# Gated MLPs of a two-block kernel: high weights against both halves of the input in 512-column products

## The chip, the cores and the metric

One core of one Trainium2 chip runs the whole program. The metric is the device time of one execution in microseconds (us), as the median of several runs; less is better. Times inside a run come from one execution that the hardware profiler recorded.

## The reference

The program computes two transformer blocks on 256 tokens of width 1024, in float32. The first has two layers of attention and squared-ReLU MLPs. The second has a gated MLP, a mixer (a state-space part beside latent attention) and another gated MLP. The two gated MLPs are what matters here:

```python
def swiglu(h, w_gate, w_up, w_down):          # h: 256 x 1024
    return (silu(h @ w_gate) * (h @ w_up)) @ w_down    # hidden width D_FF_2 = 2816
x = x + 0.5 * g1 * swiglu(modulate(rmsnorm(x, ...), sh1, sc1), ffn1_w_gate, ffn1_w_up, ffn1_w_down)
...
x = x + 0.5 * g3 * swiglu(modulate(rmsnorm(x, ...), sh3, sc3), ffn2_w_gate, ffn2_w_up, ffn2_w_down)
```

## The kernel before

**Split numbers.** TensorE multiplies in the type fp32r. To keep float32 accuracy, each operand is split into a high part (rounded to fp32r) and a low part (the rest), and a product is the sum of three: high weight with high input, high weight with low input, low weight with high input. The input's halves stand in `ah` and `al`, 8 tiles of 128 channels by 256 tokens each.

**Units.** Weights stream through in units of 1 MB (128 partitions by 2048 values) in a ring of three slots. The sync engine loads a unit into `raw` (`load`), ScalarE copies it into `whi` (`split`, L610), VectorE subtracts for `wlo` (`split`, L1065). A unit's slot is used again when TensorE has counted up `w_used`. Each engine works through its own queue in the order written.

**A gated MLP** (`swiglu` in each of the three engines' programs) has 11 chunks of 256 hidden channels. A chunk has a gate unit, an up unit and a down unit, and TensorE takes them in the order gate(j+1), up(j+1), down(j). A gate or up unit is an `a_unit`: 2 blocks of 128 output channels (m) by 8 input tiles (c) by 3 products, each of 256 columns, into one bank of PSUM (8 banks of 512 values per partition); the two blocks are the halves of that bank. Gate and up of one chunk go into banks 4 and 5, those of the next chunk into 6 and 7. The first gate and up unit are `entry_unit` and `up_unit`, which start on parts of the input. The down unit is `d_unit` (L1949, L1951, L1953): 24 products of 512 columns, in which weights are streamed and parts of h stand still, alternating between two banks; the last two down units are `last_pair` (L1913), which finishes one bank after another.

**Between the units** (`chunk`): ScalarE takes Silu of the gate bank into `hr` (L826); VectorE multiplies it with the up bank into `hs` (L1418); ScalarE copies `hs` to the high part `hh` (L828); VectorE subtracts for the low part `hl` (L1423), which releases the down unit. On both engines this stands between the weight splits of the following units: gate(j+2)'s before it, up's and down's behind it. In the first gated MLP VectorE also does the last norm of the first block (`final_norm`, written behind the first two chunks) and, two chunks on, the angles of the mixer (`angles`).

`gained` writes `ah` and `al` at the entry of a stage, with casts (L1144) and subtractions (L1145) of two tiles at once.

Of the kernel before, what the change touches and what calls it, by code (L numbers as in the profile page):

```python
# [15 lines left out]
P = 128  # L16
# [94 lines left out]
def build(nc, t_in, out):  # L111
    g = t_in
    with ExitStack() as ctx:
        def sb(name, shape, dt=F32):
            return ctx.enter_context(nc.sbuf_tensor(name, shape, dt))

        def sem(name):
            return ctx.enter_context(nc.semaphore(name))
# [3 lines left out]
        wlo = sb("wlo", [P, RING, UNIT], F32R)  # L122
        x = sb("x", [P, TT, D])
        xn = sb("xn", [P, TT, D])
        ah = sb("ah", [P, CT, S], F32R)
        al = sb("al", [P, CT, S], F32R)
        bh = sb("bh", [P, CT, S], F32R)
        bl = sb("bl", [P, CT, S], F32R)
        hh = sb("hh", [P, MLP_BODY, 2, S], F32R)
# [34 lines left out]
        place = sb("place", [P, 32 + 2 * 96])  # L164
        ps = ctx.enter_context(nc.psum_tensor("ps", [P, 8, 512], F32))

        wflat = work[:]
        hr = wflat[:, 0:512]
        hs = wflat[:, 512:1024]
# [29 lines left out]
        rope = wflat[:, 1024:2048].rearrange("p (k n) -> p k n", k=4)  # L199
        rB = gB[:, 0:S]  # L200
        rdiag = wflat[:, 1024:1024 + S].rearrange("p (t n) -> p t n", t=TT)
        fscr = st[:, 0:4096].rearrange("p (k n) -> p k n", k=8)
        nac = sm[:, 7, :].rearrange("p (t h) -> p t h", t=TT)

# [65 lines left out]
        pv_done = sem("pv_done")  # L270
        o_ready = sem("o_ready")
        gated = sem("gated")
        h_sq = sem("h_sq")
        half_tr = sem("half_tr")
        half_hi = sem("half_hi")
# [90 lines left out]

        def bank(b, n=512):
            return ps[:, b, 0:n]

        def banks(b, n):  # L370
            return ps[:].rearrange("p b n -> p (b n)")[:, 512 * b:512 * b + n]
# [229 lines left out]
        def _(act):  # L601
# [132 lines left out]
            def plain(h0, j, dst):  # L734

                act.wait_ge(pv_done, h0 + 4 * (j + 1))
                A.activation(dst.rearrange("p c n -> p (c n)"), bank(4 + j % 2), ACT.Copy).then_inc(in_hi, 1)

            def head_exp(hg, h, src, scale):
                act.wait_ge(maxed, hg + 1)  # L740
# [77 lines left out]
            def chunk(cs, used_units, b, silu, buf):  # L818
# [10 lines left out]
                else:  # L829
                    A.activation(hr, bank(b), ACT.Relu).then_inc(gated, 1)  # L830
                    act.wait_ge(gated, cs1)
                    A.activation(hh[:, buf].rearrange("p c n -> p (c n)"), hr, ACT.Square).then_inc(h_hi, 1)

            def mlp(n0, c0):
                def body(i):
                    for j in range(MLP_BODY):
                        chunk(i * MLP_BODY + (c0 + j), up_end(n0, i, j, 2, MLP_BODY), 4 + j, False, j)
                        for q in range(2):
                            n = n0 + 2 * j + 2 + q
                            split(n if isinstance(i, int) else (n, i), slot(n))  # L840
                body(0)
                with act.Fori(1, (CH1 - 1) // MLP_BODY) as i:
                    body(i)
                done[0] = n0 + N_MLP
                chunk(c0 + CH1 - 1, n0 + 2 * (CH1 - 1), 4, False, 0)

            def swiglu(n0, c0):
                def body(i):
                    for j in range(FFN_BODY):
                        n = n0 + 3 * j + 2  # L850
                        n_at = lambda q: n + q + 3 * FFN_BODY * i if isinstance(i, int) else (n + q, i)
                        split(n_at(0), slot(n))
                        used = n0 + 3 * (FFN_BODY * i + j) + 1 if isinstance(i, int) and i else up_end(n0, i, j, 3, FFN_BODY)
                        chunk(i * FFN_BODY + (c0 + j), used, 4 + 2 * j, True, j)
                        for q in (1, 2):
                            split(n_at(q), slot(n + q))
                body(0)
                if n0 == U_FFN1:
                    body(1)
                    act.wait_ge(ang_done, 1)  # L860
                    A.activation(trig[:, 3], trig[:, 2], ACT.Sin).then_inc(trig_done, 1)
                with act.Fori(2 if n0 == U_FFN1 else 1, (CH2 - 1) // FFN_BODY) as i:
                    body(i)
                done[0] = n0 + N_FFN - 1
                splits(n0 + N_FFN - 1)
                chunk(c0 + CH2 - 1, n0 + 3 * (CH2 - 1) + 1, 4, True, 0)

            col = lambda tab, cols, name, off=0: (lambda c: tab[:, cols[name] + off + c:cols[name] + off + c + 1])

# [178 lines left out]
        def _(dve):  # L1048
# [73 lines left out]
            def flat(a):  # L1122
                return a.rearrange("p c n -> p (c n)")

            def gained(stage_name, hi, lo, gain, shift=None, npairs=4, bank_of=TBANK, ntiles=CT, first=0):

                for j in range(first, npairs):
                    if stage_name in TILE and j == 0:
                        dve.wait_ge(tile_hi, TILE[stage_name] + 1)
                        first_tile(hi, lo, 0).then_inc(tile_ready, 1)  # L1130
                        dve.wait_ge(in_hi, PAIR0[stage_name] + 1)
                        first_tile(hi, lo, 1).then_inc(in_ready, 1)
                        continue
                    dve.wait_ge(in_hi, PAIR0[stage_name] + j + 1)
                    if stage_name == "mix" and j == 0:
                        ins = half_split(1)
                    elif shift is None:
                        for q in range(min(2, ntiles - 2 * j)):
                            c = 2 * j + q
                            src = ps[:, bank_of[j], q * S:(q + 1) * S]  # L1140
                            ins = V.scalar_tensor_tensor(lo[:, c], src, gain(c), hi[:, c].bitcast(F32),
                                                         ALU.mult, ALU.subtract)
                    else:
                        link(V.tensor_copy(flat(hi[:, 2 * j:2 * j + 2]), tmp2[:, j % 2]))  # L1144
                        ins = V.tensor_tensor(flat(lo[:, 2 * j:2 * j + 2]), tmp2[:, j % 2],  # L1145
                                              flat(hi[:, 2 * j:2 * j + 2]).bitcast(F32), ALU.subtract)
                    ins.then_inc(in_ready, 1)

            def first_tile(hi, lo, c):
# [11 lines left out]

            def plain(stage_name, j, hi, lo):
                dve.wait_ge(in_hi, PAIR0[stage_name] + j + 1)
                V.tensor_tensor(flat(lo), bank(4 + j % 2), flat(hi).bitcast(F32), ALU.subtract).then_inc(in_ready, 1)

            def qk_copy(n0, m):

# [244 lines left out]
            def chunk(cs, b, silu, buf):  # L1412
# [9 lines left out]
                dve.wait_ge(h_hi, cs + 1)  # L1422
                V.tensor_tensor(flat(hl[:, buf]), hs, flat(hh[:, buf]).bitcast(F32), ALU.subtract).then_inc(h_ready, 1)  # L1423

            def mlp(n0, c0, b0, nb):
                def body(i, with_ada=True):
                    k = 0
                    for j in range(MLP_BODY):
                        chunk(i * MLP_BODY + (c0 + j), 4 + j, False, j)
                        for q in range(2):  # L1430
                            u = n0 + 2 * j + 2 + q
                            split(u + 2 * MLP_BODY * i if isinstance(i, int) else (u, i), slot(u))
                            for _ in range((2, 2, 1)[j] if q else (1, 1, 1)[j]):
# [12 lines left out]

            def swiglu(n0, c0):
                def body(i):
                    for j in range(FFN_BODY):
                        u = n0 + 3 * j + 2  # L1450
                        u_at = lambda q: u + q + 3 * FFN_BODY * i if isinstance(i, int) else (u + q, i)
                        split(u_at(0), slot(u))
                        chunk(i * FFN_BODY + (c0 + j), 4 + 2 * j, True, j)
                        for q in (1, 2):
                            split(u_at(q), slot(u + q))
                body(0)
# [5 lines left out]
                    body(i)  # L1462
                done[0] = n0 + N_FFN - 1
                splits(n0 + N_FFN - 1)
                chunk(c0 + CH2 - 1, 4, True, 0)

            def ada_add(b, c):

# [344 lines left out]
        def _(pe):  # L1813
# [384 lines left out]

            def swiglu(n0, c0, stage_name, gates):

                def pair(u, i, cs, b, name=None):
                    if not isinstance(cs, int) or cs - c0 >= FFN_BODY:
                        pe.wait_ge(h_sq, cs - (FFN_BODY - 1))
                    a_unit(u if i is None else (u, i), slot(u), b, ah, al, name)
                    a_unit(u + 1 if i is None else (u + 1, i), slot(u + 1), b + 1, ah, al)

                last = (CH2 - 1) // FFN_BODY - 1

                def body(i):
                    st_ = isinstance(i, int)  # L2210
                    for j in range(FFN_BODY):
                        u = n0 + 2 + 3 * j + (3 * FFN_BODY * i if st_ else 0)
                        pair(u, None if st_ else i, i * FFN_BODY + (c0 + j + 1), 4 + 2 * ((j + 1) % FFN_BODY))
                        if st_ and i == last and j == FFN_BODY - 1:
                            last_pair((u + 2, slot(u + 2), hh[:, j], hl[:, j], 0),
                                      (u + 3, slot(u + 3), hh[:, 0], hl[:, 0], 0),
# [278 lines left out]
```

## Time and profile before

| | |
|---|---|
| median of 3 runs | 1212.42 us (1212.23 to 1212.66) |
| profiled execution | 1212.66 us, its span 1211.0 us |
| TensorE matmuls, busy | 97% of the span |
| TensorE weight loads, busy | 89% |
| VectorE (DVE), busy | 69% |
| ScalarE (ACT), busy | 49% |
| first gated MLP | about 633 to 821 us |
| second gated MLP | about 1014 us to the end |

PE is TensorE's matmuls, PEld its weight loads, DVE VectorE, ACT ScalarE. Matmuls are pipelined and the ends of their rows are modelled, so the rows overlap: the time from one start to the next is what a matmul costs in a stream, not its duration. L1839 is line 1839 of the kernel.

### The profile page before, as it was taken

The page shows a single profiled execution, that of the slowest core. Times are in us where ns is not written, and L with a number is a line of the kernel's source. Part 1 is how long each engine was busy: PE and PEld are TensorE (multiplying, and loading weights), DVE is VectorE, ACT ScalarE, POOL GpSimd, SP SyncE. Part 2 cuts the span into 40 slices and gives each one's busy share as a digit, 9 for nine tenths or more (in the row PEclk, how much of TensorE's full clock was granted, in tenths as well). Part 3 has the DMA queues.
Part 4 walks back from the last instruction along what each step waited for, and adds up shares of the span by engine and source line. Part 5 has one row for each costly group of instructions (what it writes and reads, how often), then busy time and mean ns, then how long its engine had stood idle before and what let it go on. Part 6 is the DMA issues. An engine that isn't in the chain of part 4 may idle for free.

```text
span 1211.0 us, 19661 instructions
## 1 busy us (share of the span) xinstructions
PE 1180.5 (97%) x7827; PEld 1072.5 (89%) x7827; DVE 838.8 (69%) x1127; ACT 598.1 (49%) x791; POOL 73.6 (6%) x111
## 2 busy tenths in 40 slices
PE   8999999999999999999999999999999999999997
PEld 8897899999889789999989999998988888999996
DVE  6676798888866669888576654457986866544545
ACT  5545544444545554444465334346756756434343
POOL 9200011110000001110000000000000000000000
PEclk9999999999999999999999999999999999999999
DMA  7633598997453259987635655544651053656560
GB/s 252 225 115 102 212 366 307 322 313 276 132 196 126 70 209 343 322 308 279 203 107 185 199 187 195 173 150 157 192 193 51 31 198 120 209 176 197 172 202 35
DMA packets 143241, 236.38 MB, mean 195 GB/s; under 512 B 6358, under 2 KB 106951, under 8 KB 143175
## 3 DMA queue, kind: packets, MB, share of 16 engines
q1 hardware_dynamic: 130402, 196.73, 48.8%
q0 software_dynamic: 10400, 37.77, 8.6%
q10 hardware_dynamic: 2372, 0.96, 0.3%
q8 instruction: 46, 0.75, 0.3%
q14 instruction: 21, 0.16, 0.0%
HBM read 234.37 MB, written 1.05 MB: 194 GB/s over the span
## 4 chain that ended last, share of the span: by engine, by line
PE 92%; DVE 4%; ACT 2%; issue 1%; POOL 0%; DVEq 0%; ACTq 0%; POOLq 0%
PE ps L1839 13%; PE ps L1841 13%; PE ps L1840 13%; PE ps L1949 10%; PE ps L1951 10%; PE ps L1953 10%; PE ps L1886 2%; PE ps L1888 2%; PE ps L1887 2%; PE ps L2038 1%; PE ps L2040 1%; PE ps L2039 1%; PE ps L2120 1%; PE ps L1973 1%; PE ps L1913 1%
## 5 line engine op out<-in xcount | busy, mean ns | idle before, releaser
L1065 DVE TENSOR_TENSOR wlo<-raw,whi 128x2048 fp32r<-128x2048 f32 (+2 forms) x185 | 417.3, 2260 | 194.3 <-ACT whi L610 193.9
L610 ACT ACTIVATE whi<-raw 128x2048 fp32r<-128x2048 f32 (+2 forms) x185 | 348.6, 1887 | 230.4 <-PE ps L1953 128.4
L1839 PE MATMUL ps<-ah,whi 128*128 128x256 f32 x1296 | 367.2, 283 | 3.3 <-DVE wlo L1538 1.4
L1840 PE MATMUL ps<-al,whi 128*128 128x256 f32 x1296 | 366.7, 283 | 0.0
L1841 PE MATMUL ps<-ah,wlo 128*128 128x256 f32 x1296 | 366.7, 283 | 0.0
L1839 PEld LDWEIGHTS ps<-ah,whi 128*128 128x128 f32 x1296 | 248.5, 192 | 6.2 <-DVE wlo L1538 1.7
L1840 PEld LDWEIGHTS ps<-al,whi 128*128 128x128 f32 x1296 | 248.6, 192 | 1.8
L1841 PEld LDWEIGHTS ps<-ah,wlo 128*128 128x128 f32 x1296 | 248.6, 192 | 0.0
L1949 PE MATMUL ps<-whi,hh 128*128 128x512 f32 x376 | 116.6, 391 | 0.0
L1951 PE MATMUL ps<-wlo,hh 128*128 128x512 f32 x376 | 116.1, 390 | 0.0
L1953 PE MATMUL ps<-whi,hl 128*128 128x512 f32 x376 | 116.0, 390 | 0.0
L1951 PEld LDWEIGHTS ps<-wlo,hh 128*128 128x128 f32 x376 | 70.6, 188 | 15.2
L1953 PEld LDWEIGHTS ps<-whi,hl 128*128 128x128 f32 x376 | 70.6, 188 | 15.0
L1477 DVE SCALAR_TENSOR_TENSOR stage<-stage,cact 128x1024 f32<-128x1024 f32 x63 | 80.7, 1280 | 0.9
L1949 PEld LDWEIGHTS ps<-whi,hh 128*128 128x128 f32 x376 | 67.6, 189 | 11.2
L830 ACT ACTIVATE work<-ps 128x512 f32<-128x512 f32 x32 | 19.2, 599 | 115.3 <-PE ps L1841 109.7
L583 POOL DMA_DIRECT2D stage<-in_w_ada_dram x72 | 38.4, 533 | 425.1 <-DVE stage L1477 175.4
L826 ACT ACTIVATE work<-ps 128x512 f32<-128x512 f32 x22 | 13.2, 599 | 84.4 <-PE ps L1841 77.6
L1423 DVE TENSOR_TENSOR hl<-work,hh 128x512 fp32r<-128x512 f32 x54 | 37.4, 692 | 18.0 <-ACT hh L828 16.9
L1418 DVE TENSOR_TENSOR work<-work,ps 128x512 f32<-128x512 f32 x22 | 15.1, 687 | 47.3 <-ACT work L826 47.3
L744 ACT ACTIVATE work<-ps,nmx 128x128 f32<-128x128 f32 x40 | 14.7, 368 | 58.5 <-DVE nmx L1187 58.4
L1949 PE MATMUL ps<-whi,ah 128*128 128x512 f32 x120 | 37.3, 381 | 0.0
(415 smaller groups left out, 1788.6 us busy)
## 6 DMA issues: line engine op xcount, KB each, us to landing
stage<-in_w_ada_dram POOLq DMA_DIRECT2D x72, 512.0 KB, 6.7
raw<-in_w_up_dram SPq DMA_DIRECT2D x32, 1024.0 KB, 6.4
raw<-in_w_down_dram SPq DMA_DIRECT2D x32, 1024.0 KB, 7.5
raw<-in_ffn_w_gate_dram SPq DMA_DIRECT2D x22, 1024.0 KB, 5.3
raw<-in_ffn_w_up_dram SPq DMA_DIRECT2D x22, 1024.0 KB, 5.3
raw<-in_ffn_w_down_dram SPq DMA_DIRECT2D x22, 1024.0 KB, 5.0
raw<-in_moba_w_qkv_dram SPq DMA_DIRECT2D x11, 1024.0 KB, 7.4
raw<-in_w_in_dram SPq DMA_DIRECT2D x10, 1024.0 KB, 5.2
```

The lines of the kernel that those rows point to most:

```text
L583: pool.dma_start(aslot[:, c % ADA_RING], ada[:, c, bass.ds(b * D, D)]).then_inc(a_landed[c % ADA_RING], 16)
L610: A.activation(whi[:, s, 0:size], raw[:, s, 0:size], ACT.Copy).then_inc(w_hi, 1)
L1065: V.tensor_tensor(wlo[:, s, 0:size], raw[:, s, 0:size], whi[:, s, 0:size].bitcast(F32), ALU.subtract).then_inc(w_lo, 1)
L1423: V.tensor_tensor(flat(hl[:, buf]), hs, flat(hh[:, buf]).bitcast(F32), ALU.subtract).then_inc(h_ready, 1)
L1477: V.scalar_tensor_tensor(aacc, v, cact[:, c:c + 1], aacc, ALU.mult, ALU.add).then_inc(a_sum, 1)
L1839: T.matmul(o, wmh, xh[:, c], start=(c == 0), stop=False)
L1840: T.matmul(o, wmh, xl[:, c], start=False, stop=False)
L1841: ins = T.matmul(o, wml, xh[:, c], start=False, stop=(c == CT - 1))
L1886: T.matmul(o, wmh, xh[:, c], start=(c == 0), stop=False)
L1949: T.matmul(o, xh[:, c, tt], wh[:, k, v:e], start=(first and k == 0), stop=False)
L1951: T.matmul(o, xh[:, c, tt], wl[:, k, v:e], start=False, stop=False)
L1953: ins = T.matmul(o, xl[:, c, tt], wh[:, k, v:e], start=False, stop=(last and k == kn - 1))
```

## The change

In both gated MLPs all gate and up units but those of the first chunk and the last are done by a new `wide_unit`. `ah` and `al` become the two halves of one tensor `a2`, side by side for each tile, so that one product of 512 columns multiplies a high weight tile with both. For each block m, the 8 high tiles come first (512 columns), then the 8 low tiles (256 columns, high input only). A block fills a whole bank: its first half collects high-high and low-high, its second half high-low. So a gate unit takes banks 6 and 7 and an up unit banks 4 and 5, in every chunk. The halves are then added: ScalarE copies the second halves of both banks to SBUF, VectorE adds the first halves to that copy, and Silu and the product read the sums in SBUF. TensorE waits for these sums (`g_sum`, `u_sum`) before it uses the banks again. The last chunk keeps the old form, in banks 6 and 7.

```diff
-        ah = sb("ah", [P, CT, S], F32R)
-        al = sb("al", [P, CT, S], F32R)
+        a2 = sb("a2", [P, CT, 2, S], F32R)
...
+        ah, al = a2[:, :, 0], a2[:, :, 1]
...
+        g_low, g_full, u_low, u_full = (st[:, 4096 + 512 * k:4608 + 512 * k] for k in range(4))
...
+        def by_c(a):
+            return a.rearrange("p (c n) -> p c n", c=2)
+
+        def both(b, half):
+            return ps[:, b:b + 2, half * S:half * S + S]
...
+            def gated_chunk(cs, k, gate_used, buf):
+
+                act.wait_ge(w_used, gate_used)
+                A.activation(by_c(g_low), both(6, 1), ACT.Copy).then_inc(g_copied, 1)
+                act.wait_ge(g_sum, k)
+                A.activation(hr, g_full, ACT.Silu).then_inc(gated, 1)
+                act.wait_ge(w_used, gate_used + 1)
+                A.activation(by_c(u_low), both(4, 1), ACT.Copy).then_inc(u_copied, 1)
+                act.wait_ge(h_sq, cs + 1)
+                A.activation(hh[:, buf].rearrange("p c n -> p (c n)"), hs, ACT.Copy).then_inc(h_hi, 1)
...
-                        used = n0 + 3 * (FFN_BODY * i + j) + 1 if isinstance(i, int) and i else up_end(n0, i, j, 3, FFN_BODY)
-                        chunk(i * FFN_BODY + (c0 + j), used, 4 + 2 * j, True, j)
+                        if isinstance(i, int) and i == 0 and j == 0:
+                            chunk(c0, n0 + 2, 4, True, 0)
+                        else:
+                            gated_chunk(i * FFN_BODY + (c0 + j), i * FFN_BODY + (k0 + j), i * (3 * FFN_BODY) + (n0 + 3 * j), j)
...
-                        link(V.tensor_copy(flat(hi[:, 2 * j:2 * j + 2]), tmp2[:, j % 2]))
-                        ins = V.tensor_tensor(flat(lo[:, 2 * j:2 * j + 2]), tmp2[:, j % 2],
-                                              flat(hi[:, 2 * j:2 * j + 2]).bitcast(F32), ALU.subtract)
+                        link(V.tensor_copy(hi[:, 2 * j:2 * j + 2], by_c(tmp2[:, j % 2])))
+                        ins = V.tensor_tensor(lo[:, 2 * j:2 * j + 2], by_c(tmp2[:, j % 2]),
+                                              hi[:, 2 * j:2 * j + 2].bitcast(F32), ALU.subtract)
...
+            def gated_chunk(cs, k, buf):
+
+                dve.wait_ge(g_copied, k)
+                V.tensor_tensor(by_c(g_full), both(6, 0), by_c(g_low), ALU.add).then_inc(g_sum, 1)
+                dve.wait_ge(u_copied, k)
+                V.tensor_tensor(by_c(u_full), both(4, 0), by_c(u_low), ALU.add).then_inc(u_sum, 1)
+                dve.wait_ge(u_sum, k)
+                dve.wait_ge(gated, cs + 1)
+                dve.wait_ge(h_ready, cs)
+                V.tensor_tensor(hs, hr, u_full, ALU.mult).then_inc(h_sq, 1)
+                dve.wait_ge(h_sq, cs + 1)
+                dve.wait_ge(h_hi, cs + 1)
+                V.tensor_tensor(flat(hl[:, buf]), hs, flat(hh[:, buf]).bitcast(F32), ALU.subtract).then_inc(h_ready, 1)
...
+                def wide_unit(n, s, b):
+
+                    unit_wait(n)
+                    wh, wl = w_view(whi, s, CT, AW), w_view(wlo, s, CT, AW)
+                    for m in range(AW // P):
+                        for c in range(CT):
+                            T.matmul(bank(b + m), wh[:, c, m * P:(m + 1) * P], a2[:, c].rearrange("p k n -> p (k n)"),
+                                     start=(c == 0), stop=False)
+                        for c in range(CT):
+                            ins = T.matmul(bank(b + m, S), wl[:, c, m * P:(m + 1) * P], ah[:, c], start=False,
+                                           stop=(c == CT - 1))
+                    ins.then_inc(w_used, 1)
+
+                def pair(u, i, k):
+                    if not isinstance(k, int) or k > 0:
+                        pe.wait_ge(g_sum, k)
+                    wide_unit(u if i is None else (u, i), slot(u), 6)
+                    if isinstance(k, int) and k == k0:
+                        pe.wait_ge(h_sq, c0 + 1)
+                    if not isinstance(k, int) or k > 0:
+                        pe.wait_ge(u_sum, k)
+                    wide_unit(u + 1 if i is None else (u + 1, i), slot(u + 1), 4)
...
+                        if st_ and i == last and j == FFN_BODY - 1:
+                            pe.wait_ge(g_sum, k0 + CH2 - 2)
+                            a_unit(u, slot(u), 6, ah, al)
+                            a_unit(u + 1, slot(u + 1), 7, ah, al)
+                        else:
+                            pair(u, None if st_ else i, i * FFN_BODY + (k0 + j))
```

## Rows read from the trace of the kernel before

**Rows 1.** The page's busy times (share of the span, instructions) and TensorE's clock:

```profile
PE 1180.5 (97%) x7827; PEld 1072.5 (89%) x7827; DVE 838.8 (69%) x1127; ACT 598.1 (49%) x791; POOL 73.6 (6%) x111
...
PEclk9999999999999999999999999999999999999999
```

**Rows 2.** The page's chain that ended last, by engine and by line:

```profile
PE 92%; DVE 4%; ACT 2%; issue 1%; POOL 0%; DVEq 0%; ACTq 0%; POOLq 0%
PE ps L1839 13%; PE ps L1841 13%; PE ps L1840 13%; PE ps L1949 10%; PE ps L1951 10%; PE ps L1953 10%; PE ps L1886 2%; PE ps L1888 2%; PE ps L1887 2%; PE ps L2038 1%; PE ps L2040 1%; PE ps L2039 1%; PE ps L2120 1%; PE ps L1973 1%; PE ps L1913 1%
```

**Rows 3.** Windows of one chunk in each gated MLP:

```profile
core 0: us, PE busy (x) PEld busy (x) DVE busy (x) ACT busy (x) POOL busy (x), PEclk, DMA share, GB/s
725.02:742.00 16.98, 16.98 (x122) 16.02 (x121) 8.26 (x5) 6.87 (x5) 0.00 (x0) 1.00 0.58 185
1072.63:1089.61 16.98, 16.98 (x123) 16.02 (x121) 8.26 (x5) 6.87 (x5) 0.00 (x0) 1.00 0.58 186
```

**Rows 4.** TensorE's timeline over one chunk (start, us, engine, line, shapes, count):

```profile
713.51 0.28 PE L1839 MATMUL ps<-ah,whi 128*128 128x256 f32 x1
...
725.02 0.63 PE L1949 MATMUL ps<-whi,hh 128*128 128x512 f32 x2
725.49 0.62 PE L1951 MATMUL ps<-wlo,hh 128*128 128x512 f32 x2
...
726.41 0.61 PE L1949 MATMUL ps<-whi,hh 128*128 128x512 f32 x2
...
730.49 0.28 PE L1839 MATMUL ps<-ah,whi 128*128 128x256 f32 x1
...
730.84 0.28 PE L1839 MATMUL ps<-ah,whi 128*128 128x256 f32 x1
```

**Rows 5.** TensorE's timeline in the last pair of the first gated MLP:

```profile
815.13 0.39 PE L1913 MATMUL ps<-whi,hh 128*128 128x512 f32 x1
...
821.02 0.39 PE L1913 MATMUL ps<-whi,hl 128*128 128x512 f32 x1
```

**Rows 6.** TensorE's timeline at the second up unit, idle time and releaser last:

```profile
650.52 0.28 PE L1841 MATMUL ps<-ah,wlo 128*128 128x256 f32 x1
651.24 0.39 PE L1839 MATMUL ps<-ah,whi 128*128 128x256 f32 x1 [0.45 <-DVE wlo L1065]
```

**Rows 7.** ScalarE's timeline in the chunk of rows 4:

```profile
725.22 0.60 ACT L826 ACTIVATE work<-ps 128x512 f32<-128x512 f32 x1 [3.85 <-PE ps L1841]
...
736.44 1.91 ACT L610 ACTIVATE whi<-raw 128x2048 fp32r<-128x2048 f32 x1 [3.84 <-PE ps L1841]
```

**Rows 8.** VectorE's timeline in the same chunk:

```profile
725.85 0.69 DVE L1418 TENSOR_TENSOR work<-work,ps 128x512 f32<-128x512 f32 x1 [2.15 <-ACT work L826]
...
729.05 2.29 DVE L1065 TENSOR_TENSOR wlo<-raw,whi 128x2048 fp32r<-128x2048 f32 x1 [1.04 <-ACT whi L610]
...
738.39 2.29 DVE L1065 TENSOR_TENSOR wlo<-raw,whi 128x2048 fp32r<-128x2048 f32 x1 [3.46 <-ACT whi L610]
```

**Rows 9.** The page's DMA issues, with KB each and us to landing:

```profile
raw<-in_ffn_w_gate_dram SPq DMA_DIRECT2D x22, 1024.0 KB, 5.3
```

**Rows 10.** VectorE's timeline around `final_norm` in the first gated MLP:

```profile
664.78 2.29 DVE L1065 TENSOR_TENSOR wlo<-raw,whi 128x2048 fp32r<-128x2048 f32 x1 [1.36 <-ACT whi L610]
...
672.93 1.28 DVE L1361 SCALAR_TENSOR_TENSOR x<-x,newt,nB 128x1024 f32<-128x1024 f32 x1
674.25 2.29 DVE L1065 TENSOR_TENSOR wlo<-raw,whi 128x2048 fp32r<-128x2048 f32 x1
```

**Rows 11.** Groups by shape: VectorE's writes of the input halves (busy, mean ns):

```profile
L1145 DVE TENSOR_TENSOR al<-work,ah 128x512 fp32r<-128x512 f32 x9 | 6.2, 692 | 0.3
L1144 DVE CAST ah<-work 128x512 fp32r<-128x512 f32 x9 | 3.8, 427 | 0.3 <-ACT work L664 0.2
```

More of the change, by code:

```diff
@@ L272, in build @@
         gated = sem("gated")
+        g_copied = sem("g_copied")
+        g_sum = sem("g_sum")
+        u_copied = sem("u_copied")
+        u_sum = sem("u_sum")
         h_sq = sem("h_sq")
@@ L736, in plain @@
                 act.wait_ge(pv_done, h0 + 4 * (j + 1))
-                A.activation(dst.rearrange("p c n -> p (c n)"), bank(4 + j % 2), ACT.Copy).then_inc(in_hi, 1)
+                A.activation(dst, by_c(bank(4 + j % 2)), ACT.Copy).then_inc(in_hi, 1)
             def head_exp(hg, h, src, scale):
@@ L847, in swiglu @@
             def swiglu(n0, c0):
+                k0 = 0 if n0 == U_FFN1 else CH2 - 2
                 def body(i):
@@ L865, in swiglu @@
                 splits(n0 + N_FFN - 1)
-                chunk(c0 + CH2 - 1, n0 + 3 * (CH2 - 1) + 1, 4, True, 0)
+                chunk(c0 + CH2 - 1, n0 + 3 * (CH2 - 1) + 1, 6, True, 0)
             col = lambda tab, cols, name, off=0: (lambda c: tab[:, cols[name] + off + c:cols[name] + off + c + 1])
@@ L1163, in plain @@
                 dve.wait_ge(in_hi, PAIR0[stage_name] + j + 1)
-                V.tensor_tensor(flat(lo), bank(4 + j % 2), flat(hi).bitcast(F32), ALU.subtract).then_inc(in_ready, 1)
+                V.tensor_tensor(lo, by_c(bank(4 + j % 2)), hi.bitcast(F32), ALU.subtract).then_inc(in_ready, 1)
             def qk_copy(n0, m):
@@ L1452, in body @@
                         split(u_at(0), slot(u))
-                        chunk(i * FFN_BODY + (c0 + j), 4 + 2 * j, True, j)
+                        if isinstance(i, int) and i == 0 and j == 0:
+                            chunk(c0, 4, True, 0)
+                        else:
+                            gated_chunk(i * FFN_BODY + (c0 + j), i * FFN_BODY + (k0 + j), j)
                         for q in (1, 2):
@@ L1464, in swiglu @@
                 splits(n0 + N_FFN - 1)
-                chunk(c0 + CH2 - 1, 4, True, 0)
+                chunk(c0 + CH2 - 1, 6, True, 0)
             def ada_add(b, c):
@@ L2199, in swiglu @@
             def swiglu(n0, c0, stage_name, gates):
[L2201 to L2205, printed above, removed]
+                def wide_unit(n, s, b):
[18 more added lines that the diff above has]
+                    wide_unit(u + 1 if i is None else (u + 1, i), slot(u + 1), 4)
+                k0 = 0 if n0 == U_FFN1 else CH2 - 2
                 last = (CH2 - 1) // FFN_BODY - 1
@@ L2212, in body @@
                         u = n0 + 2 + 3 * j + (3 * FFN_BODY * i if st_ else 0)
-                        pair(u, None if st_ else i, i * FFN_BODY + (c0 + j + 1), 4 + 2 * ((j + 1) % FFN_BODY))
+                        if st_ and i == last and j == FFN_BODY - 1:
+                            pe.wait_ge(g_sum, k0 + CH2 - 2)
+                            a_unit(u, slot(u), 6, ah, al)
+                            a_unit(u + 1, slot(u + 1), 7, ah, al)
+                        else:
+                            pair(u, None if st_ else i, i * FFN_BODY + (k0 + j))
                         if st_ and i == last and j == FFN_BODY - 1:
```

1 line of the change is left out of this document (added).

## The prediction

> **What bounds the kernel now.** I read the page's busy table and slices first [rows 1]: TensorE's matmuls are busy for 97% of the span and its granted clock is at the top digit in all 40 slices, so this kernel runs at the 2.4 GHz level throughout; VectorE has 69%, ScalarE 49%. A busy TensorE can still be one that waits, so I read the chain that ended last [rows 2]: 92% of it is TensorE, and the three lines of `a_unit` have 13% each. Then the windows of one chunk in the two gated MLPs [rows 3]: both take 16.98 us, TensorE is busy for all of it, VectorE for 8.26 and ScalarE for 6.87 us, the clock is 1.00, and DMA has 0.58. So in the steady chunk TensorE's own stream sets the time, and only a shorter stream helps.
>
> The timeline of TensorE over one chunk gives the price of the stream [rows 4]. Matmul rows show pipelined durations (0.28 us for 256 columns), which overlap, so I go by starts. The gate and up units run from 713.51 to 725.02: 11.51 us for 96 matmuls of 256 columns, 119.9 ns each; I use 120.0, the regular step between rows. From 726.41 to 730.49, 18 matmuls of 512 columns take 4.08 us: 226.7 ns each. Two of 256 cost 240.0, one of 512 costs 226.7. With streaming at 2.4 GHz (106.7 and 213.3 ns) that leaves 13.3 ns for each instruction, whatever its width. The change halves the number of instructions for the same columns. There is also a cost of switching widths: the first six 512-column matmuls after a run of 256 take 1.39 us (725.02 to 726.41), 0.03 more than six at 226.7; back at 256, the first three take 0.35 (730.49 to 730.84), 0.01 less than 0.36.
>
> **TensorE's stream.** A unit has 2 blocks of output channels (m) and 8 input tiles (c). Before: 16 x 3 = 48 matmuls of 256. After: 16 of 512 (high weight with high and low input at once) and 16 of 256 (low weight with high input). The columns stay 12,288. A pair (gate and up) goes from 96 x 0.1200 = 11.52 us to 32 x 0.2267 + 32 x 0.1200 = 7.254 + 3.840 = 11.094 us, 0.426 less. The four changes of width from 512 down, and up again, are now within the pair: before, a chunk switched up once (into the down unit) and down once; after, it switches up four times and down four times. Three more of each cost 3 x (0.03 - 0.01) = 0.06. The pair then saves 0.366 us. Each weight tile has its own load in both versions; the loads drop from 96 to 64 a pair, behind longer matmuls.
>
> A wide product adds to the same 512 columns of one bank eight times running, while the down unit of [rows 4] alternates between two banks. `last_pair` shows that this costs nothing: from 815.13 to 821.02 it makes 26 steps, each group of 12 into one bank, in 5.89 us, 226.5 ns each [rows 5].
>
> There are 11 chunks in each gated MLP; the first pair and the last keep the old form, so 9 x 2 = 18 pairs change: 18 x 0.366 = 6.6 us.
>
> **Where TensorE is not the bound.** In the first wide pair of each MLP the up unit waits for its low weights: its predecessor's last matmul starts at 650.52, it starts at 651.24 after a wait for VectorE [rows 6]. The splits before it are not touched, so a gate unit that ends 0.18 us earlier only waits 0.18 us longer: half of that pair's gain is lost, twice: 0.36 us. This leaves 6.2 us.
>
> **ScalarE and VectorE.** Each changed chunk adds two ScalarE copies (low halves of gate and up to SBUF) of 0.60 us, by the activation that reads 512 elements from PSUM now [rows 7], and two VectorE additions of 0.69 us, by its product with a PSUM operand [rows 8]. The Silu stays, but reads SBUF. ScalarE goes to about 6.87 + 1.20 = 8.1 us, VectorE to 8.26 + 1.38 = 9.6 us, of a chunk of 16.6: no bound by throughput. So it is a question of who waits:
> - Gate side. The gate unit ends at 736.25 (730.49 + 5.76). ScalarE's split of the next gate starts at 736.44 and takes 1.91 [rows 7], then comes the new copy, 0.60. VectorE's split of 2.29 starts at 738.39 [rows 8], ends at 740.68, and then comes the addition: the gate sum is there at 741.4, 5.15 us after the gate unit. TensorE asks for it only at its next gate unit, after an up and a down unit: 5.58 + 5.47 = 11.05 us. Slack 5.9. The Silu follows at about 5.15 to 5.8, when the up unit ends (5.58), so it delays the up copy by nothing to 0.1 us.
> - Up side. ScalarE begins 0.20 us after the up unit's end (725.22 against 725.02), and today the split of the next up unit ends at 729.05 + 2.29 = 731.34, 6.32 us after it [rows 7, 8]. What is queued behind the new waits on both engines is the end of this chunk (the product, the two halves of h) and that split. Copy and addition come in, 1.29, and the Silu goes out, 0.60: 7.0 us. TensorE wants the unit after a down and a gate unit, 11.05 us: slack 4.0. The up banks' sum is there at 1.6, also wanted at 11.05. The down unit's h comes later by 0.7 with the same slack.
> - DMA. A slot of raw weights comes free when VectorE has split it (740.68 above for a gate unit), now up to 0.8 us later for an up unit. ScalarE splits the next content of that slot one chunk after 736.44, at about 753: 12 us for a load that lands in 5.3 [rows 9]. It stays hidden.
>
> The Trainium skill, Perfetto Trace Analysis, "Matmuls", says that independent groups should rotate through PSUM banks so that the evacuation of one overlaps the next group's matmuls. This change gives up that rotation between chunks: gate always in banks 6 and 7, up in 4 and 5. By the page alone it would cost; by the two sums above it has 5.9 and some 9 us of cover, and I price it at 0.
>
> One chunk has less slack. In the first gated MLP, `final_norm` stands in VectorE's queue between two chunks: a split at 664.78, then small operations up to the one of 1.28 us at 672.93, then the gate split at 674.25 [rows 10]. Shifted by 0.3 us: free at 673.9, gate split to 676.2, gate sum 676.9, Silu 677.5, up copy 678.1, up sum 678.8, product 679.5, high half 680.1, ScalarE's split of up to 682.1, VectorE's to 684.35. TensorE: the down unit starts 0.18 + 0.37 = 0.55 us before the window's bound 674.08, at 673.5, then 5.47 + 5.58: it wants up at 684.55. That is a tie within 0.2 us. I take 0.1, bounds 0 and 1.0 us (handoffs at eight places). This leaves 6.1 us.
>
> **The layout.** `ah` and `al` become views of one tensor with 512-element steps. Every read by TensorE is still 128 or 256 contiguous values. VectorE's casts of 512 elements take 0.43 us, faster than its two-operand 0.69 [rows 11]; if the split destination took that away, 9 x 0.26 = 2.3 us would be added, most of it in the entry of an MLP, where TensorE spends 12 x 0.120 = 1.44 us on a pair of tiles and VectorE then 0.69 + 0.69 = 1.38. I take 0, with 0.5 as a bound. The first and last chunks, other stages and the tail after the last pair keep their instructions.
>
> **Sum.** The profiled execution took 1212.66 us (span 1211.0, 1.7 around it), 0.24 above the median of the runs. Minus 6.1 it is 1206.55; from the median, **1206.3 us**.
>
> **The rivals.**
> A. The excess isn't one per instruction: a wide product of this kind costs what two narrow ones do, 240 ns. The gain is 0: 1212.4. The down unit and `last_pair`, at 226.7 and 226.5, speak against it; for it only that both stream weights, and this streams activations. 6%.
> B. A smaller fixed cost than 13.3 ns: the steps of 120.0 and 226.7 would have to hide something other than a cost per instruction, and the gain would be small, between 0 and 2.4 us: about 1211. 3%. The Trainium skill, TensorE: Matmul & The Clock Gate, "Back-to-back issue gap", gives N / 2.4 + 2.5 ns for an isolated warm matmul. By that 18 x 32 x 2.5 ns = 1.4 us would be saved, 1211.0 in all. The steps of this trace are 11 ns above it at both widths, so the row decides here.
> C. The new handoffs take TensorE's place: g_sum, u_sum or the next up split come late in the steady chunk. It decides from a lengthening of 4.0 us on the up side beyond my 0.7. At 0.2 us a pair beyond that: 18 x 0.2 = 3.6 us given back, 1209.9. 8%.
> D. The other side: wide products slower than 226.7 because eight run straight after a switch, in contention with more PSUM reads. If all went at the pace of the first two after a switch (725.02 to 725.49 in [rows 4], 0.47 us for two, 235 ns each), a pair would save 0.426 - 0.266 = 0.16, in all 2.9 less 0.4: 1209.9. It ends slower by over 0.2% only from about 242 ns, 15 above the row: 18 x 32 x 15 ns = 8.7 us lost of 6.1 gained: 1215. Mild 2%, slower 5%.
> E. Weight loads were a hidden part of the 120 ns, and halving their rate gives more: 1204 or less. 2%.
>
> **How the numbers follow.** The forecast has 74%. Its own range: the best is no switch cost and no tie lost, 18 x 0.426 - 0.4 = 7.3, 1205.1; the worst is 0.03 a switch with nothing back, 18 x 0.336 - 0.36 - 1.0 - 0.5 = 4.2, 1208.2. The whole range takes in C, the mild form of D and some of E: 1204.6 to 1209.9. 0.2% is 2.4 us and about what can be told from no change here: faster is below 1210.0. Faster 0.83 (forecast, E, mild D, 5 of C's 8 in 100), same 0.11 (A, B, 2 of C's), slower 0.06 (the rest of D and C).
>
> **What would show it.** Right: a steady chunk of 16.6 us in place of 16.98, TensorE busy for all of it, wide products 226 to 228 ns apart and narrow 120; no waits of TensorE on VectorE's sums; the first up unit still starting after a wait. Wrong: steps of the wide products at 235 or more (A, D), idle TensorE ahead of a gate or up unit with VectorE as releaser (C), the tie after `final_norm` lost by over 1 us, or longer casts at an MLP's entry.

## The result, and the profile after

| kernel | median | profiled execution | its span |
|---|---|---|---|
| before (5 runs beside the change) | 1212.66 us | 1212.66 us | 1211.0 us |
| changed (5 runs, 1206.25 to 1206.73) | 1206.62 us | 1206.32 us | 1204.7 us |

The quotient of the two medians is 0.9950; the ratio on record is 0.9939, with a 95% interval of 0.9911 to 0.9967, so the change is faster beyond the noise. Forecast were 1206.3 us and a gain of 6.1; measured are 1206.6 and 6.0. Some executions of several kernels, the one before among them, took about 10 us more at a mean granted clock of 0.989 instead of 0.998; the medians below are over all executions, and the profile of the run with the early split is of such a one (1213.66 us), with a clock of 1.00 up to 940 us and so in the rows shown.

The page of the changed kernel gives busy times, share of the span and number of instructions for each engine, and the clock in 40 slices. It answers to [rows 1]:

```profile
PE 1172.8 (97%) x7251; PEld 1041.0 (86%) x7251; DVE 862.4 (72%) x1163; ACT 617.8 (51%) x827; POOL 73.4 (6%) x111
...
PEclk9999999999999999999999999999999999999999
```

TensorE has 576 matmuls and as many weight loads fewer (18 pairs by 32), VectorE and ScalarE 36 instructions more each. TensorE is still busy for 97%.

The windows of one chunk answer to [rows 3]. The first is the chunk behind `final_norm`, the others are steady ones of the first and the second gated MLP:

```profile
core 0: us, PE busy (x) PEld busy (x) DVE busy (x) ACT busy (x) POOL busy (x), PEclk, DMA share, GB/s
673.26:689.88 16.62, 16.62 (x91) 14.34 (x89) 12.88 (x10) 8.21 (x8) 0.00 (x0) 1.00 0.49 158
723.10:739.72 16.62, 16.62 (x91) 14.34 (x89) 9.56 (x7) 7.99 (x8) 0.00 (x0) 1.00 0.55 189
1068.42:1085.03 16.61, 16.61 (x90) 14.33 (x89) 9.56 (x7) 7.99 (x8) 0.00 (x0) 1.00 0.56 190
```

A chunk takes 16.62 us where it took 16.98, TensorE is busy throughout, and VectorE and ScalarE have the 1.3 and 1.1 us more that two additions and two copies cost. TensorE's timeline over the same chunk answers to [rows 4]; runs of one form are merged, with their count last:

```profile
728.57 1.98 PE L2252 MATMUL ps<-a,whi 128*128 128x512 f32 x8
730.39 1.11 PE L2255 MATMUL ps<-a,wlo 128*128 128x256 f32 x8
731.34 2.00 PE L2252 MATMUL ps<-a,whi 128*128 128x512 f32 x8
733.18 1.11 PE L2255 MATMUL ps<-a,wlo 128*128 128x256 f32 x8
```

From start to start: eight wide products straight after the down unit take 1.82 us (728.57 to 730.39), 227 ns each. Eight after a narrow run take 1.84 (731.34 to 733.18), 230 each. Eight narrow ones take 0.95, 119 each. A long run of 512 has 226.7 for each, so a switch up costs 0.03 (1.84 less 8 x 0.2267), and the way back gives 0.01 (0.96 less 0.95). Both steps of the sum, and the cost of a switch, are there as they were priced.

### The profile page after: what moved, and what is told of

It reads as the page before. It is cut to its first block, busy times and chain, and to the rows that moved or that the text cites. A ratio compares the mean times of both kernels' runs of the same rounds, so it can differ in the third digit from the quotient of the medians.

```text
span 1204.7 us, 18596 instructions
## 1 busy us (share of the span) xinstructions
PE 1172.8 (97%) x7251; PEld 1041.0 (86%) x7251; DVE 862.4 (72%) x1163; ACT 617.8 (51%) x827; POOL 73.4 (6%) x111
## 4 chain that ended last, share of the span: by engine, by line
PE 92%; DVE 4%; ACT 2%; issue 1%; POOL 0%; DVEq 0%; ACTq 0%; POOLq 0%
PE ps L2252 10%; PE ps L1994 10%; PE ps L1996 10%; PE ps L1998 10%; PE ps L1884 7%; PE ps L1886 7%; PE ps L1885 7%; PE ps L2255 5%; PE ps L1931 2%; PE ps L1933 2%; PE ps L1932 2%; PE ps L2083 1%; PE ps L2085 1%; PE ps L2084 1%; PE ps L2165 1%
## 5 line engine op out<-in xcount | busy, mean ns | idle before, releaser
L1884 PE MATMUL ps<-a,whi 128*128 128x256 f32 x720 | 204.1, 283 | 3.2 <-DVE wlo L1583 2.2
L1886 PE MATMUL ps<-a,wlo 128*128 128x256 f32 x720 | 203.7, 283 | 0.0
L1885 PE MATMUL ps<-a,whi 128*128 128x256 f32 x720 | 203.7, 283 | 0.0
L2252 PE MATMUL ps<-a,whi 128*128 128x512 f32 x576 | 144.0, 392 | 1.4 <-DVE wlo L1091 1.4
L1884 PEld LDWEIGHTS ps<-a,whi 128*128 128x128 f32 x720 | 138.0, 192 | 5.0 <-DVE wlo L1583 2.4
L1885 PEld LDWEIGHTS ps<-a,whi 128*128 128x128 f32 x720 | 138.0, 192 | 1.2
L1886 PEld LDWEIGHTS ps<-a,wlo 128*128 128x128 f32 x720 | 138.1, 192 | 0.0
L2252 PEld LDWEIGHTS ps<-a,whi 128*128 128x128 f32 x576 | 104.6, 189 | 21.2 <-issue 1.8
L2255 PEld LDWEIGHTS ps<-a,wlo 128*128 128x128 f32 x576 | 78.6, 190 | 5.6
L2255 PE MATMUL ps<-a,wlo 128*128 128x256 f32 x576 | 80.3, 282 | 0.0
L841 ACT ACTIVATE work<-ps 128x512 f32<-128x512 f32 x32 | 19.2, 599 | 114.7 <-PE ps L1886 109.1
```

The costliest lines, as they stand in the source:

```text
L1884: T.matmul(o, wmh, xh[:, c], start=(c == 0), stop=False)
L1885: T.matmul(o, wmh, xl[:, c], start=False, stop=False)
L1886: ins = T.matmul(o, wml, xh[:, c], start=False, stop=(c == CT - 1))
L2252: T.matmul(bank(b + m), wh[:, c, m * P:(m + 1) * P], a2[:, c].rearrange("p k n -> p (k n)"), start=(c == 0), stop=False)
L2255: ins = T.matmul(bank(b + m, S), wl[:, c, m * P:(m + 1) * P], ah[:, c], start=False, stop=(c == CT - 1))
```

## The experiments

The changed kernel is the base of the first three, of the two with a late product, and of the one in the other MLP. Times are medians; the kernel before ran beside each batch, at 1212.60 and 1212.61 us. The ratios are those on record; they are not the quotients of the medians (for the early split that would be 0.9929), so steps of a microsecond between two runs are read from the medians.

| run | median, us | ratio on record (95%) |
|---|---|---|
| narrow products, new evacuation | 1212.69 | 1.0004 (0.9984 to 1.0024) |
| wide and narrow alternate | 1209.51 | 0.9975 (0.9965 to 0.9984) |
| two runs of widths in a unit | 1205.71 | 0.9944 (0.9931 to 0.9957) |
| the same, second up split early | 1204.03 | 0.9942 (0.9921 to 0.9963) |
| one late product | 1213.51 | 1.0003 (0.9987 to 1.0019) |
| two late products | 1235.14 | 1.0181 (1.0166 to 1.0197) |
| wide in a squared-ReLU MLP | 1218.69 | 1.0051 (1.0036 to 1.0067) |
| last gate unit wide as well | 1203.52 | 0.9924 (0.9911 to 0.9938) |

### Only the width undone

```diff
                         for c in range(CT):
-                            T.matmul(bank(b + m), wh[:, c, m * P:(m + 1) * P], a2[:, c].rearrange("p k n -> p (k n)"),
-                                     start=(c == 0), stop=False)
+                            T.matmul(bank(b + m, S), wh[:, c, m * P:(m + 1) * P], ah[:, c], start=(c == 0), stop=False)
+                            T.matmul(ps[:, b + m, S:2 * S], wh[:, c, m * P:(m + 1) * P], al[:, c], start=False,
+                                     stop=False)
```

> Only the width is undone: each high tile meets the two input halves in two products of 256 columns, into the same banks, in the same order (high tiles first, then low), with the new copies and sums kept. My theory (the gain is one fixed cost of 13.3 ns per instruction, the evacuation is free): a pair goes back to 96 x 0.120 = 11.52 us, the steady chunk to 16.98, the whole to about 1212.5 us, the time of the kernel before. Rival (the gain comes from the order of tiles or from gate and up having fixed banks): it stays near 1206.6. Rival (the extra copies and sums cost something that the width hides): above 1213.

Measured: 1212.69 us. Windows of the steady chunk in both MLPs, of this kernel:

```profile
724.71:741.69 16.98, 16.98 (x123) 16.02 (x121) 9.56 (x7) 7.99 (x7) 0.00 (x0) 1.00 0.55 186
1072.31:1089.29 16.98, 16.98 (x122) 16.02 (x121) 9.55 (x7) 7.99 (x7) 0.00 (x0) 1.00 0.55 187
```

TensorE's numbers are those of [rows 3] to the hundredth, while VectorE and ScalarE have those of the changed kernel. So the new copies and sums (the evacuation of the banks), the fixed banks and the order of tiles together cost and give nothing; the whole gain is the width. Each product keeps its own weight load here too, so this run does not tell whether the 13.3 ns belong to the product or to its load.

### Wide and narrow in turns

```diff
                         for c in range(CT):
                             T.matmul(bank(b + m), wh[...], a2[:, c]..., start=(c == 0), stop=False)
-                        for c in range(CT):
                             ins = T.matmul(bank(b + m, S), wl[...], ah[:, c], start=False, stop=(c == CT - 1))
```

> Only the order within a unit changes: each high tile's 512-column product is followed by the low tile's 256-column product, so the width switches 16 times a unit, where it switched twice. Theory (a switch up and down costs 0.027 - 0.008 = 0.019 us, each time, by the steps in the trace of the changed kernel): 14 more in each of 36 units, 36 x 14 x 0.019 = 9.7 us, so 1216.3 us, slower than the kernel before. Rival (the extra steps of 233, 236, 228, 233, 231 ns belong to the start of a run and its first five or six products, and a single wide product does not pay them in full): one wide product pays at most its first step, 234 instead of 227, and the narrow one 113 instead of 120; 1206 to 1208 us.

Measured: 1209.51 us, between what the theory and its rival gave, and in neither's range. TensorE's timeline, one row for each product:

```profile
699.84 0.40 PE L2252 MATMUL ps<-a,whi 128*128 128x512 f32 x1
700.08 0.28 PE L2254 MATMUL ps<-a,wlo 128*128 128x256 f32 x1
...
701.61 0.40 PE L2252 MATMUL ps<-a,whi 128*128 128x512 f32 x1
701.85 0.28 PE L2254 MATMUL ps<-a,wlo 128*128 128x256 f32 x1
701.96 0.40 PE L2252 MATMUL ps<-a,whi 128*128 128x512 f32 x1
```

Six wide and six narrow take 2.12 us (699.84 to 701.96), 353 ns for two, where the steady steps sum to 346.7. A switch up and down costs 6.6 ns if the run is one product long, not 19. For a pair that is 32 x 0.0066 = 0.21 us, less the 0.06 to 0.08 of the four switches it had: 0.15, and the chunk is 16.79 for 16.62, 0.17 more. 18 x 0.17 = 3.1, the measured loss is 2.9. My theory was too simple: a switch into a run of one costs a third of a switch into a run of eight, so the cost builds up over the first products of a run. The rival had that, but took the single wide product for cheaper than it is. The order in the change, a run of eight and then another, is worth half its gain.

### Fewer switches

```diff
                     for m in range(AW // P):
                         for c in range(CT):
                             T.matmul(bank(b + m), wh[...], a2[:, c]..., start=(c == 0), stop=False)
+                    for m in range(AW // P):
                         for c in range(CT):
                             ins = T.matmul(bank(b + m, S), wl[...], ah[:, c], start=False, stop=(c == CT - 1))
```

> Both banks' high tiles first (16 wide products), then both banks' low tiles (16 narrow): two switches up in a chunk instead of four. Theory (0.019 us for each switch up and down): 18 x 2 x 0.019 = 0.7 us less, steady chunk 16.58 instead of 16.62, 1205.9 us. Rival (switches cost only what the run before them saved, or the cost is tied to a change of bank): the chunk stays at 16.62 and the time at 1206.6.

Measured: 1205.71 us, 0.9 under the changed kernel. Windows of two steady chunks:

```profile
723.05:739.63 16.58, 16.58 (x91) 14.35 (x90) 9.55 (x7) 8.00 (x8) 0.00 (x0) 1.00 0.59 191
1068.06:1084.63 16.57, 16.57 (x90) 14.34 (x89) 9.55 (x7) 7.99 (x8) 0.00 (x0) 1.00 0.58 190
```

0.04 a chunk, as priced, and the executions of the two kernels do not overlap (1205.61 to 1206.02 against 1206.25 to 1206.73): with runs of eight or more, the cost is one per switch.

### The second up unit's weights earlier

The gain of the first changed pair was half lost to a wait. In `swiglu`'s first body, on ScalarE and in the same way on VectorE:

```diff
                         split(n_at(0), slot(n))
                         if isinstance(i, int) and i == 0 and j == 0:
+                            split(n_at(1), slot(n + 1))
                             chunk(c0, n0 + 2, 4, True, 0)
...
-                        for q in (1, 2):
+                        for q in (2,) if isinstance(i, int) and i == 0 and j == 0 else (1, 2):
                             split(n_at(q), slot(n + q))
```

> As the run with two runs of widths in a unit, and in the first body of both gated MLPs the second up unit's weights are split before chunk 0's Silu and products on ScalarE and VectorE, which were idle there for 3 us and more. Theory: the second up unit no longer waits; the step ahead of it was 0.99 us, 0.77 more than a narrow product's 0.12 plus what a switch leaves, so 0.8 to 0.9 us in each MLP, 1.6 us together: 1204.3 us. Rival (something else is late next: the sum of chunk 0 or the gate unit): the wait moves and the gain is under 0.5 us, 1205.4 or more.

Measured: 1204.03 us, 1.7 less than without it. TensorE's timeline, of the changed kernel first, then of this one:

```profile
649.52 0.76 PE L2255 MATMUL ps<-a,wlo 128*128 128x256 f32 x5
650.99 0.93 PE L2252 MATMUL ps<-a,whi 128*128 128x512 f32 x3 [0.71 <-DVE wlo L1091]
```

```profile
649.52 1.12 PE L2258 MATMUL ps<-a,wlo 128*128 128x256 f32 x8
650.48 0.63 PE L2254 MATMUL ps<-a,whi 128*128 128x512 f32 x2
```

The wait is gone and nothing took its place there.

### How much slack the evacuation has

```diff
+                for q in range(1):       # 2 in the second run
+                    V.tensor_tensor(st[:, 2048 * q:2048 * q + 2048], x[:].rearrange("p t n -> p (t n)"),
+                                    x[:].rearrange("p t n -> p (t n)"), ALU.mult)
                 V.tensor_tensor(hs, hr, u_full, ALU.mult).then_inc(h_sq, 1)
```

> The changed kernel with one VectorE product of 2048 elements (about 2.3 us, its result is not used) ahead of each changed chunk's gated product, so that the high and low halves of h and the split of the next up unit come 2.3 us later. Theory (slack of 3.85 us in the steady chunk, read from the changed trace: the split ends 7.18 us after the up unit, wanted at 11.03; and 0.2 us in the one chunk after the last norm of the first block): the steady chunk stays at 16.61 us, TensorE waits once for about 2.1 us, 1208.7 us in all. Rival (the new evacuation is already close to setting the time everywhere): some us or more in each of 18 chunks, 1215 us or more. Rival (no tie at the norm's chunk): 1206.6.

Measured: 1213.51 us, with single executions from 1211.98 to 1214.85; the profiled one took 1214.82. The steady chunk agrees, the sum doesn't, and neither rival has it. Windows of this kernel, one steady chunk and then the stretch behind `final_norm`:

```profile
748.27:764.89 16.62, 16.62 (x91) 14.35 (x90) 11.66 (x8) 7.88 (x8) 0.00 (x0) 1.00 0.56 189
```

```profile
684.60:688.20 3.60, 0.24 (x3) 0.03 (x1) 2.56 (x3) 3.60 (x3) 0.00 (x0) 0.89 0.00 0
688.20:690.00 1.80, 1.79 (x4) 1.50 (x5) 1.80 (x1) 1.72 (x2) 0.00 (x0) 0.50 0.32 56
690.00:692.00 2.00, 2.00 (x6) 1.53 (x5) 2.00 (x2) 0.00 (x0) 0.00 (x0) 0.50 1.03 357
692.00:694.00 2.00, 2.00 (x10) 1.90 (x10) 1.16 (x2) 0.63 (x1) 0.00 (x0) 0.50 1.08 397
694.00:696.00 2.00, 2.00 (x11) 1.72 (x10) 0.00 (x0) 0.00 (x0) 0.00 (x0) 0.95 1.01 377
```

The columns are length, busy time of TensorE, its loads, VectorE, ScalarE and GpSimd, granted clock, DMA share and GB/s. TensorE's timeline there:

```profile
688.21 3.78 PE L2255 MATMUL ps<-a,whi 128*128 128x512 f32 x8 [3.38 <-DVE wlo L1091]
691.79 1.91 PE L2258 MATMUL ps<-a,wlo 128*128 128x256 f32 x8
```

TensorE waits 3.4 us, not 2.1: the extra product delays `final_norm` too, so it counts nearly twice in that chunk. The granted clock falls before the wait is over (the mean of the idle stretch is 0.89) and is 0.50, the 1.2 GHz level, when TensorE goes on, until about 694. That chunk takes 22.96 us (673.65 to 696.61), 6.3 more: 3.5 from the step that holds the wait, and the other 2.8 are the products at half clock. The chunk of `angles` lost another 1.8, which I had not priced; 6.3 and 1.8 make up the 8.2 us by which the profiled execution is above the changed kernel. So the tie behind `final_norm` is one that a single further operation would have lost, and a wait of that length took the clock with it.

> The same with two such products (about 4.6 us): past the slack of 3.85. Theory: TensorE now waits in each steady chunk. By the chain from up unit to up unit the period is 7.18 + 4.6 + 5.58 = 17.3 us; the loop through ScalarE and VectorE alone (up copy, sums, two products, h, three splits, gate sum, Silu) gives 17.5. So 17.3 to 17.6 us a chunk against 16.61, and 1222 to 1228 us in all. Rival (the slack is larger than read, or the load hides it): 16.61 and about 1211 us.

Measured: 1235.14 us. A steady chunk, and where TensorE waits in it:

```profile
1109.69:1127.05 17.36, 16.87 (x90) 14.39 (x89) 13.77 (x9) 7.87 (x7) 0.00 (x0) 1.00 0.53 182
```

```profile
1121.36 2.11 PE L2255 MATMUL ps<-a,whi 128*128 128x512 f32 x8 [0.49 <-DVE wlo L1091]
```

The period is the chain from up unit to up unit, and the releaser is the split of the up weights. That the sum of the expectation (7.18 + 4.6 + 5.58) gives just 17.36 is in part luck. Read from rows, the two products add 4.4 us, not 4.6; the split ends 11.6 us after the up unit, TensorE goes on at 11.67 (1109.69 to 1121.36), and its up unit takes 5.69 us instead of 5.58 (1121.36 to 1127.05), because the first product after the wait takes 0.1 longer. The slack of 3.85 us agrees with both runs: 2.2 us more changes nothing, and 4.4 brings a wait of 0.6 us (11.67 for 11.03). The total is over my 1228 through the same two special chunks, 26.4 and 24.2 us here.

### The same in a squared-ReLU MLP

Up units of chunks 1 to 15 of the first block's first MLP; the core of the edit on VectorE:

```diff
+            def relu_chunk(c, buf):
+
+                dve.wait_ge(m_copied, c)
+                V.tensor_tensor(by_c(g_full), both(6, 0), by_c(g_low), ALU.add).then_inc(m_sum, 1)
+                dve.wait_ge(gated, c + 1)
+                dve.wait_ge(h_ready, c)
+                V.tensor_tensor(hs, hr, hr, ALU.mult).then_inc(h_sq, 1)
```

> The changed kernel with wide products also in the up units of chunks 1 to 15 of the first squared-ReLU MLP, into banks 6 and 7, with a ScalarE copy and a VectorE sum before the ReLU. TensorE's stream alone would save 15 x 0.18 = 2.7 us: 1203.9 us. My theory is another: VectorE is busy there for 9.35 of 11.22 us a chunk and has forced idle time; 0.69 more and the wait for copy and ReLU make it the bound, 11.5 to 12.3 us a chunk, 4 to 16 us lost: 1211 to 1223 us.

Measured: 1218.69 us, 12 more than the changed kernel and within the 1211 to 1223 of the theory. Windows of two chunks there, of the changed kernel and then of this one:

```profile
235.74:246.96 11.22, 11.22 (x75) 10.26 (x73) 9.04 (x8) 4.96 (x4) 1.06 (x2) 1.00 0.81 282
246.96:258.18 11.22, 11.22 (x75) 10.26 (x73) 9.55 (x8) 4.95 (x4) 1.59 (x3) 1.00 0.91 334
```

```profile
240.72:252.75 12.03, 11.32 (x59) 9.34 (x58) 10.12 (x9) 5.48 (x5) 1.06 (x2) 1.00 0.73 262
252.75:264.18 11.43, 11.31 (x59) 9.34 (x57) 9.61 (x9) 5.47 (x5) 1.58 (x3) 1.00 0.88 321
```

```profile
247.06 2.12 PE L2251 MATMUL ps<-a,whi 128*128 128x512 f32 x8 [0.71 <-DVE stage L1486]
```

TensorE is busy for 11.32 of 12.03 us and waits for VectorE's sum; VectorE stands at 10.12 with forced idle time around it. ScalarE's copy starts at 240.92, 0.2 us after the up unit, but the sum starts at 246.27: a split and three operations on `stage` stand ahead of it in VectorE's queue, and TensorE wants the banks back after a down unit, 5.5 us. So one bank pair and a VectorE that is 81 to 85% busy are together enough to turn the gain round. Which share is whose is not shown, for no run gives these units a second bank pair. The two chunks lose 1.0 us, which would be about 8 over 15 chunks; another 2.7 us is a wait of TensorE for the last chunk's low half of h, and the rest of the 12 I did not trace.

### The last gate unit wide

The last chunk's gate unit, added to the version with the early split; its Silu leaves the end of the chain:

```diff
-                            a_unit(u, slot(u), 6, ah, al)
-                            a_unit(u + 1, slot(u + 1), 7, ah, al)
+                            wide_unit(u, slot(u), 6)
+                            pe.wait_ge(u_sum, k0 + CH2 - 2)
+                            a_unit(u + 1, slot(u + 1), 4, ah, al)
```

> The run with two runs of widths and the early second split, and the last chunk's gate unit wide too, so that its sum and Silu are done while the last up unit runs, whose product VectorE then takes from PSUM at once. Theory: the wide gate unit saves 0.18 us in each MLP; of the Silu's 0.63 us, which stood on the chain that ends each MLP, about 0.3 us each comes off, since the first half of the down unit before it ends only 0.3 us later: 1.0 us together, 1203.1 us. Rival (the whole Silu comes off): 1202.4. Rival (TensorE's end isn't what the last norm waits for): 1204.0.

Measured: 1203.52 us, 0.5 less than without it (1203.12 to 1203.55 against 1203.68 to 1204.07), half of what I expected, and the best version: 9.1 us under the kernel before. Against the run with two runs of widths, from the last full down unit of the first gated MLP to the mixer's first is 67.55 us, where it was 68.33: 0.78 less, more than the 0.5 priced for one MLP. At the second, VectorE's first operation on the last pair's result comes 4.41 us after that pair begins, where it took 4.82. Some of it is lost at the end: the last store of the output is issued at 1197.71, and the span ends 4.2 us later, where it was 3.3 (1200.80 to 1204.1). Why that store lands later I did not settle.

## Why the prediction was right, point by point

The mechanism held, not only the number. The measured terms are 18 x 0.36 us for the pairs and 2 x 0.27 lost at the first pairs, 5.9 us together, for a forecast of 6.6, 0.36 and 0.1 for the tie. The small misses nearly cancel, which is luck. The time is 0.3 us over the forecast mostly because the forecast starts from a median of 1212.42 us, and the kernel before had 1212.66 beside the change.

**What bounds the kernel** held: the chunk is TensorE's stream before and after, and the run with narrow products shows that nothing else moved.

**TensorE's stream** was sized right: 0.426 less 0.06 forecast, 16.98 - 16.62 = 0.36 found. The switch cost, taken from one transition in [rows 4], is the same at each of the four in the changed chunk, and two of them can be saved. "Whatever its width" is shown for 256 and 512 only; the last section has a width for which it does not hold.

**Accumulating into one bank** costs nothing for eight in a row, as [rows 5] had it.

**Where TensorE is not the bound.** The wait ahead of the second up unit stayed, 0.71 us idle for the 0.45 of [rows 6]. I had half of each first pair's gain lost, 0.18 us. The step that holds the wait grew from 0.72 to 0.99 us, so it was 0.27: all that the gate unit gained and 0.1 more. The early split shows that the wait was worth 0.85 us in each MLP.

**ScalarE and VectorE.** Sizes of the new operations: the copy 0.57 to 0.60, the sum 0.68 to 0.69. The next up split ends 7.2 us after the up unit (7.0 forecast). Here are VectorE's rows of the changed kernel behind `final_norm`, to be held against [rows 10]:

```profile
672.50 1.28 DVE L1387 SCALAR_TENSOR_TENSOR x<-x,newt,nB 128x1024 f32<-128x1024 f32 x1
673.82 2.29 DVE L1091 TENSOR_TENSOR wlo<-raw,whi 128x2048 fp32r<-128x2048 f32 x1
676.03 0.68 DVE L1454 TENSOR_TENSOR stage<-ps,stage 128x512 f32<-128x512 f32 x1
677.90 0.69 DVE L1456 TENSOR_TENSOR stage<-ps,stage 128x512 f32<-128x512 f32 x1 [1.19 <-ACT stage L852]
...
681.82 4.49 DVE L1091 TENSOR_TENSOR wlo<-raw,whi 128x2048 fp32r<-128x2048 f32 x2 [1.04 <-ACT whi L621]
```

```profile
684.29 0.63 PE L2252 MATMUL ps<-a,whi 128*128 128x512 f32 x2
```

The first of the two splits ends at about 684.07 (4.49 / 2 after 681.82), and the up unit starts at 684.29 without a wait: the tie was won by 0.2 us, as worked out (684.35 and 684.55). I took 0.1 for it and it cost 0. Its bound of 1.0 us left the clock out: a wait of 3.4 us there lost clock as well, in the run with one late product. Whether a wait of 1 us would have is not shown; one of 1.56 us elsewhere did not.

**The layout.** The casts stay at 0.43 us with their new destination:

```profile
L1170 DVE CAST a<-work 128x512 fp32r<-128x512 f32 x9 | 3.8, 427 | 0.3 <-ACT work L675 0.2
```

The Trainium skill, VectorE: DVE Perf Modes, "What auto-detection actually checks", gives the condition for the two-port mode of a one-source operation: source and destination in SBUF, with outermost dimensions (of more than one element) that are both even or equal. The new destination has an outermost dimension of two, with runs of 256, and the source is read in the same form. The trace agrees with that rule: 427 ns before and after.

**The rivals.** A and B are refuted by the steps of 227 and 119 ns in the changed trace: the 13 ns are one per instruction at 256 as at 512 columns. Whether they belong to the product or to its weight load no run tells, since every product here has a load of its own. C needs 3.85 us more on the up side, and the late products show it sets in where it should. D did not come: the widest steps are those at a switch, and no run of wide products stays there. E did not come either: the steps equal those of before.

## What to carry to other kernels

Where matmuls run back to back, price a stream by the steps between starts of each width, not by rows' durations; here each instruction carried 13.3 ns at 2.4 GHz, so halving the count of narrow products pays, and long runs of one width pay a little again. The operations that the wider form adds elsewhere are free only while the engine that does them has slack in its queue at that point: the same edit gained 6 us in one kind of MLP and lost 12 in the other. Work out the one chunk with extra work in the queue, for it decides whether the slack is real.

## What the hardware showed that I had not expected

- The 13.3 ns of each matmul is only there at the upper clock. At the granted clock of 0.50 in the run with one late product, 8 narrow products take 1.71 us (691.79 to 693.50), 214 ns each, and that is 256 / 1.2 GHz with nothing over; wide ones step by 427 (688.81 to 691.37, six steps). By these steps the change would have saved nothing at that level. The Trainium skill, TensorE: Matmul & The Clock Gate, "Back-to-back issue gap", has the same form for an isolated matmul, nothing over at 1.2 GHz and a fixed part at 2.4, but 2.5 ns for it; the trace has 13.3 for each load and matmul of this type.
- TensorE stood idle for 3.4 us behind `final_norm` in that run, and the clock was at 1.2 GHz as it went on, for nearly 6 us; the stall of 1.56 us in the chunk of `angles` brought no such fall (the next wide step is 0.34 us, then 0.23 as ever).
- The cost of a switch from 256 to 512 columns builds up over some products: 6.6 ns up and down for runs of one, 19 for runs of eight and of sixteen.
- Neither figure carries over to a narrower product. In the mixer of the kernel before, products of 512 and 176 columns alternate. Each of these rows holds one of each, though it names the form of the first alone:

```profile
831.56 0.51 PE L1949 MATMUL ps<-whi,ah 128*128 128x512 f32 x2
...
833.27 0.51 PE L1953 MATMUL ps<-whi,al 128*128 128x512 f32 x2
```

Five such pairs take 1.71 us, 342 ns each. 226.7 and 176 / 2.4 + 13.3 would make 313, so there are 29 ns over, and the cause is open.
